# First normalisation in tile groups with an on-chip spread of the condition, and shorter sums of squares at two later norms

## The reference, cut to what matters

```python
mod = silu(c) @ w_ada[l] + b_ada[l]
sh_m, sc_m, gt_m, sh_f, sc_f, gt_f = jnp.split(mod, 6, axis=-1)
h = rms_norm(x, g_mix[l]) * (1.0 + sc_m) + sh_m
proj = jnp.einsum('bsd,de->bse', h, w_in[l])
```

## Time and profile before

| | us |
|---|---|
| median of 3 runs | 795.64 (795.53 to 795.8) |
| the profiled execution, its own time | 795.57 |
| its span | 793.8 |
| PE busy | 751.9 (95%) |
| DVE busy | 649.1 (82%) |
| ACT busy | 387.9 (49%) |
| first matmul of lin 0 starts | 37.61 |

### The profile page before, as it was taken

The page is one execution under the profiler, slowest core; times in us unless marked ns, Lnnn a source line. Parts: engine busy times, 40 slices in busy tenths (PEclk is TensorE's granted clock), DMA queues, the critical chain, the costliest instruction groups (busy, mean ns, idle before and its releaser), DMA issues.

```text
span 793.8 us, 13124 instructions
## 1 busy us (share of the span) xinstructions
PE 751.9 (95%) x5479; PEld 697.9 (88%) x5480; DVE 649.1 (82%) x1001; ACT 387.9 (49%) x521; POOL 46.2 (6%) x31
## 2 busy tenths in 40 slices
PE   0499999999999999999999999999999999999996
PEld 0399999999999999999999998888778899999995
DVE  3988767995897799999898779999989956987752
ACT  2355645557547654544547532322463335365742
POOL 0000000000000422223222000000000000000000
PEclk9799999999999999999999999999999999999998
DMA  9999998765563557766645241313106643563101
GB/s 347 417 352 365 368 348 311 264 223 198 206 240 136 208 212 251 273 246 247 258 175 197 91 176 53 107 55 104 54 0 235 224 148 118 225 231 118 54 1 54
DMA packets 26086, 156.58 MB, mean 197 GB/s; under 512 B 2691, under 2 KB 7084, under 8 KB 7852
## 3 DMA queue, kind: packets, MB, share of 16 engines
q1 hardware_dynamic: 21392, 148.91, 50.5%
q10 hardware_dynamic: 4636, 6.85, 2.6%
HBM read 154.68 MB, written 1.06 MB: 196 GB/s over the span
## 4 chain that ended last, share of the span: by engine, by line
PE 84%; DVE 9%; ACT 3%; issue 1%; ACTq 1%; POOL 1%; DVEq 0%
PE psum L1344 71%; DVE w_lo L832 4%; PE psum L1379 2%; DVE w_lo L865 2%; PE psum L1636 1%; PE psum L1810 1%; PE psum L1786 1%; ACT w_hi L371 1%; PE psum L1798 1%; PE psum L1622 1%; PE psum L1486 1%; DVE arena L1034 1%; DVE arena L1039 0%; PE psum L1601 0%; PE psum L1471 0%
## 5 line engine op out<-in xcount | busy, mean ns | idle before, releaser
L1344 PE MATMUL psum<-h_hi,w_hi 128*128 128x256 f32 (+1 forms) x1312 | 397.2, 303 | 10.2 <-DVE h_lo L905 9.2
L1344 PE MATMUL psum<-h_lo,w_hi 128*128 128x256 f32 (+1 forms) x1312 | 392.1, 299 | 0.0
L1344 PE MATMUL psum<-h_hi,w_lo 128*128 128x256 f32 (+1 forms) x1312 | 392.1, 299 | 0.0
L1344 PEld LDWEIGHTS psum<-h_hi,w_hi 128*128 128x128 f32 x1312 | 251.1, 191 | 21.8 <-issue 11.6
L1344 PEld LDWEIGHTS psum<-h_lo,w_hi 128*128 128x128 f32 x1312 | 251.5, 192 | 7.8 <-issue 0.2
L1344 PEld LDWEIGHTS psum<-h_hi,w_lo 128*128 128x128 f32 x1312 | 251.3, 192 | 7.4
L865 DVE TENSOR_TENSOR w_lo<-raw,w_hi 128x2048 fp32r<-128x2048 f32 x93 | 212.7, 2288 | 50.2 <-ACT w_hi L371 49.4
L371 ACT CAST w_hi<-raw 128x2048 fp32r<-128x2048 f32 x93 | 176.9, 1905 | 20.6 <-DMA raw<-in_w 16.3
L832 DVE SCALAR_TENSOR_TENSOR w_lo<-raw,cond 128x1024 fp32r<-128x1024 f32 x88 | 119.5, 1395 | 8.3 <-PE psum L1344 7.5
L832 DVE SCALAR_TENSOR_TENSOR w_lo<-raw,arena 128x1024 fp32r<-128x1024 f32 x48 | 56.8, 1221 | 0.8
L336 POOL TENSOR_TENSOR arena<-arena 128x512 f32<-128x512 f32 x11 | 26.1, 2370 | 372.9 <-ACT arena L588 372.9
(11 more groups left out here) (214 smaller groups left out, 783.7 us busy)
## 6 DMA issues: line engine op xcount, KB each, us to landing
raw<-in_w SPq DMA_DIRECT2D x141, 1024.0 KB, 4.9
xs<-in_xs ACTq DMA_DIRECT2D x2, 1024.0 KB, 12.0
consts<-diff ACTq DMA_DIRECT2D x8, 128.0 KB, 5.5
cond<-in_cond ACTq DMA_DIRECT2D x1, 1024.0 KB, 6.4
out<-xs SPq DMA_DIRECT2D x4, 256.0 KB, 2.4
arena<-in_cond ACTq DMA_DIRECT2D x1, 512.0 KB, 6.8
consts<-in_c ACTq DMA_DIRECT2D x1, 512.0 KB, 3.4
arena<-in_c ACTq DMA_DIRECT2D x1, 448.0 KB, 3.2
```

The lines of the kernel that those rows point to most:

```text
L1344: last = mm(out, w[a], x[b], start=start and n == 0, stop=stop and n == 2, skip_group_check=skip)
```

## The change

Five things are changed.

1. **Condition.** All three conditions come as one row of 12 KB in one partition. PE spreads them to all partitions by fp32 matmuls with a row of ones (`spread`, 512 columns each). The first two wait for this load and go to banks 0 and 1; ACT applies Silu from there. ACT applies Silu to the other two conditions in the row; four more matmuls spread them later and ACT copies them out. The two broadcast loads (0.5 MB and 1 MB) are gone, and so is a later Silu over 128x2048 with a reload of the function table.
2. **Loads.** ACT's queue issues the condition alone. `xs`, `vec` in two parts, `rel`, `onehot` and `c0` are issued by SP between the chunks; the block of ones is set by POOL. Storing and reloading the position biases moves to after lin 2 and lin 4.
3. **Order.** The mod chunks of scale and shift alternate, one pair for two tiles. `ORDER` begins mod 0 to 3, lin 0, mod 4, mod 5, lin 1, mod 6, mod 7, and goes on as before from lin 2. DVE norms tiles 0 to 3, then 4 and 5, then 6 and 7, and PE takes lin 0 and lin 1 in the pieces tiles 0 to 5 of both, then 6 and 7 of both. 14 bf16 matmuls of zeros (512 columns) stand after the first spread on PE, 14 more before lin 0.
4. **Sums.** For `odd_ctx` DVE adds the squares of tiles 0 to 5 in pairs and PE makes 3 sums in place of 6. For the last norm DVE adds the squares of tiles 0 to 5 into one, and PE makes 3 sums in place of 8, all behind tile 7's matmuls.
5. **Last scaling.** Three multiplies of 3, 3 and 2 tiles in place of eight, and three stores.

```diff
+HEAD = MOD_FIRST + 2
 N_MOD = 48
 LIN_OPEN = 1
-
-ADA_SC_M, ADA_SH_M, ADA_GT_M, ADA_SH_F, ADA_SC_F, ADA_GT_F = 0, 4, 8, 12, 16, 20
+LAST_PARTS = ((0, 3), (3, 6), (6, 8))
+
+ADA_SC_M, ADA_SH_M, ADA_GT_M, ADA_SH_F, ADA_SC_F, ADA_GT_F = 0, 1, 8, 12, 16, 20
...
-    order = [("lin", 0)] + [("mod", m) for m in range(MOD_FIRST)]
+    order = [("mod", m) for m in range(4)] + [("lin", 0), ("mod", 4), ("mod", 5), ("lin", 1), ("mod", 6), ("mod", 7)]
     m = MOD_FIRST
-    for j in range(LIN_BR + 3):
-        order += [("lin", j)] if j else []
+    for j in range(2, LIN_BR + 3):
+        order += [("lin", j)]
...
+        cond_row, ones_row = arena[0:1, 0:3 * D], arena[0:1, 3 * D:3 * D + P]
...
+                if r == 2:
+                    sp.dma_start(xs[:, :, 0:T], xs_d[:, :, 0:T]).then_inc(sem("x_loaded"), 16)
+                elif r == 4:
+                    sp.dma_start(vec[:, 0:VEC["g_ffn"]], vec_d[:, 0:VEC["g_ffn"]]).then_inc(sem("vec_loaded"), 16)
+                elif r == 12:
+                    sp.dma_start(c0[:, 0:P], c0_d).then_inc(sem("c0_loaded"), 16)
+                    sp.dma_start(vec[:, VEC["g_ffn"]:N_VEC], vec_d[:, VEC["g_ffn"]:N_VEC]).then_inc(sem("vec_loaded"), 16)
+                elif r == 6:
+                    sp.dma_start(rel[0:32, :], rel_d).then_inc(sem("rel_loaded"), 16)
+                    sp.dma_start(onehot, c1_d[0:33, 512:896]).then_inc(sem("rel_loaded"), 16)
                 load(r, r % RAW, ORDER[r - RAW] if r >= RAW else None)
 
-            for q in range(4):
-                sp.wait_ge(sem("last_done"), 2 * (q + 1))
-                sp.dma_start(out_d[:, 2 * q:2 * q + 2, :], xs[:, 2 * q:2 * q + 2, 0:T]).then_inc(sem("stored"), 16)
-            sp.wait_ge(sem("stored"), 64)
+            for q, (a, b) in enumerate(LAST_PARTS):
+                sp.wait_ge(sem("last_done"), q + 1)
+                sp.dma_start(out_d[:, a:b, :], xs[:, a:b, 0:T]).then_inc(sem("stored"), 16)
+            sp.wait_ge(sem("stored"), 16 * len(LAST_PARTS))
...
+            pool.memset(c0[:, P:2 * P], 1.0).then_inc(sem("ones_set"), 1)
...
-            act.dma_start(cond_ada, bass.AP(cond_d.tensor, 0, [[0, P], [1, D]])).then_inc(sem("cond_ada_loaded"), 16)
-            act.dma_start(rel[0:32, :], rel_d).then_inc(sem("rel_loaded"), 16)
-            act.dma_start(onehot, c1_d[0:33, 512:896]).then_inc(sem("rel_loaded"), 16)
-            act.dma_start(xs[:, :, 0:T], xs_d[:, :, 0:T]).then_inc(sem("x_loaded"), 16)
-            act.dma_start(c0[:, :], c0_d).then_inc(sem("c0_loaded"), 16)
-            act.dma_start(vec[:, :], vec_d).then_inc(sem("vec_loaded"), 16)
+            act.dma_start(cond_row, bass.AP(cond_d.tensor, 0, [[0, 1], [1, 3 * D]])).then_inc(sem("cond_loaded"), 16)
...
-            act.wait_ge(sem("cond_ada_loaded"), 16)
-            nc.scalar.activation(cond_ada, cond_ada, ACT.Silu).then_inc(sem("cond_ada_ready"), 1)
-            split(0)
-
-            act.wait_ge(sem("bias_row"), 1)
-            nc.scalar.copy(urow, bank[3][0:8, 0:384]).then_inc(sem("bias_row_out"), 1)
-            act.wait_ge(sem("bias_row_out"), 1)
-            act.dma_start(diff_d, urow).then_inc(sem("bias_stored"), 16)
-            act.wait_ge(sem("bias_stored"), 16)
-
+            for n in range(2):
+                act.wait_ge(sem("cond_spread"), n + 1)
+                nc.scalar.activation(cond_ada[:, 512 * n:512 * (n + 1)], bank[n], ACT.Silu).then_inc(sem("cond_ada_ready"), 1)
+            nc.scalar.activation(cond_row[:, D:3 * D], cond_row[:, D:3 * D], ACT.Silu).then_inc(sem("cond_row_ready"), 1)
             def load_trev(h):
 
                 act.dma_start(trev[:, h % TREV, :], bass.AP(diff_d.tensor, 384 * h, [[1, P], [1, T]])
                               ).then_inc(sem(f"trev_loaded{h % TREV}"), 16)
 
-            for h in range(TREV):
-                load_trev(h)
             act.wait_ge(sem("eps_set"), 2)
             load_ln_exp()
             act.wait_ge(sem("x_loaded"), 16)
             for k in range(KT):
                 square("mix", k)
             rstd_of("mix")
-            shift_hi("mix")
+            shift_hi("mix", range(4))
+            split(0)
+            split(1)
+            for v in range(2):
+                act.wait_ge(sem("cond_spread"), 4 + 2 * v)
+                nc.scalar.copy(cond[:, v, :], wide[:, 2 * v:2 * v + 2, :].rearrange("p b n -> p (b n)")
+                               ).then_inc(sem("cond_ready"), 1)
+            shift_hi("mix", (4, 5))
+            split(2)
+            shift_hi("mix", (6, 7))
 
             act.dma_start(consts[:, 0:512], c1_d[:, 0:512]).then_inc(sem("c1_loaded"), 16)
-            split(1)
-
-            act.dma_start(cond.rearrange("p v n -> p (v n)"),
-                          bass.AP(cond_d.tensor, D, [[0, P], [1, 2 * D]])).then_inc(sem("cond_loaded"), 16)
+
             for j in range(LIN_GATE):
-                split(j + 2)
-                if j == 6:
-                    act.wait_ge(sem("cond_loaded"), 16)
-                    nc.scalar.activation(cond[:, :, :], cond[:, :, :], ACT.Silu).then_inc(sem("cond_ready"), 1)
-                    load_ln_exp()
+                if j:
+                    split(j + 2)
...
+                if j == 2:
+                    act.wait_ge(sem("bias_row"), 1)
+                    nc.scalar.copy(urow, bank[3][0:8, 0:384]).then_inc(sem("bias_row_out"), 1)
+                    act.wait_ge(sem("bias_row_out"), 1)
+                    act.dma_start(diff_d, urow).then_inc(sem("bias_stored"), 16)
+                if j == 4:
+                    act.wait_ge(sem("bias_stored"), 16)
+                    for h in range(TREV):
+                        load_trev(h)
...
+            def first_mods(pair):
+
+                for m in range(2 * pair, 2 * pair + 2):
+                    mod(m, RAW_OF_MOD[m] % RAW, 16 * (RAW_OF_MOD[m] // RAW + 1), 2, 2)
+
+            def first_scaled(p0, p1, done, count):
+
+                mod_bias(2 * p0, 2 * p1)
+                n = p1 - p0
+                at = VEC["g_mix"] + 2 * p0
+                scale = modv[:, 8 * p0:8 * p1].rearrange("p (q m t v) -> p q m t v", m=2, t=2, v=2)[:, :, 0, :, 0]
+                out, gain = (z.rearrange("p (q t) -> p q t", t=2) for z in (coef[:, 2 * p0:2 * p1], vec[:, at:at + 2 * n]))
+                nc.vector.scalar_tensor_tensor(out, scale, 1.0, gain, ALU.add, ALU.mult).then_inc(sem(done), 1)
+                dve.wait_ge(sem(done), count)
+                dve.wait_ge(sem("rstd_ready"), 1)
+                for k in range(2 * p0, 2 * p1):
+                    nc.vector.scalar_tensor_tensor(norm_tmp[:, k, :], xs[:, k, 0:T], coef[:, k:k + 1], rstd[:, 0:T],
+                                                   ALU.mult, ALU.mult).then_inc(sem("normed"), 1)
+
+            def first_lo(p0, p1):
+
+                for k in range(2 * p0, 2 * p1):
+                    dve.wait_ge(sem("norm_hi"), k + 1)
+                    nc.vector.scalar_tensor_tensor(h_lo[:, k, 0:T], norm_tmp[:, k, :], shift_col(ADA_SH_M, k),
+                                                   h_hi[:, k, 0:T].bitcast(F32), ALU.add,
+                                                   ALU.subtract).then_inc(sem("norm_lo"), 1)
+
+            dve.wait_ge(sem("cond_ada_ready"), 2)
+            first_mods(0)
+            first_mods(1)
+            dve.wait_ge(sem("vec_loaded"), 16)
+            first_scaled(0, 2, "mix_coef", 1)
+            first_lo(0, 2)
+            mod(4, RAW_OF_MOD[4] % RAW, 16 * (RAW_OF_MOD[4] // RAW + 1), 2, 2)
             split(0)
-            dve.wait_ge(sem("cond_ada_ready"), 1)
-            for m in range(MOD_FIRST):
-                mod(m, RAW_OF_MOD[m] % RAW, 16 * (RAW_OF_MOD[m] // RAW + 1), 1, 1)
-            dve.wait_ge(sem("vec_loaded"), 16)
-            mod_bias(0, 8)
-            coefficients(0, "g_mix", mod_row(ADA_SC_M, 0))
-            norm("mix", 1)
+            mod(5, RAW_OF_MOD[5] % RAW, 16 * (RAW_OF_MOD[5] // RAW + 1), 2, 2)
+            first_scaled(2, 3, "mix_coef", 2)
             split(1)
+            first_lo(2, 3)
+            first_mods(3)
+            first_scaled(3, 4, "coef_ready", 1)
+            first_lo(3, 4)
...
+            for k in (0, 2, 4):
+                dve.wait_ge(sem("sq_odd_ctx"), k + 2)
+                nc.vector.tensor_tensor(gain_sq[:, k, :], gain_sq[:, k, :], gain_sq[:, k + 1, :],
+                                        ALU.add).then_inc(sem("odd_ctx_added"), 1)
...
+            def add_squares(ks):
+
+                for k in ks:
+                    dve.wait_ge(sem("sq_last"), k + 1)
+                    if k > 1:
+                        dve.wait_ge(sem("last_added"), k - 1)
+                    nc.vector.tensor_tensor(norm_tmp[:, 0, :], norm_tmp[:, 0, :], norm_tmp[:, k, :],
+                                            ALU.add).then_inc(sem("last_added"), 1)
...
+                    if k == 3:
+                        add_squares((1,))
+                    if k == 5:
+                        add_squares((2, 3))
+                    if k == 6:
```

(56 more changed lines are left out.)

20 lines of the change are left out of this document (13 added, 7 removed).

## The result

| | before | changed |
|---|---|---|
| median of 4 runs, us | 795.67 (795.53 to 795.8) | 784.45 (784.32 to 785.16) |
| ratio, 95% interval | | 0.9859 [0.9847, 0.9871] |
| the profiled execution / its span, us | 795.57 / 793.8 | 784.45 / 782.6 |
| first mod product of DVE | 15.44 | 8.23 |
| first matmul of lin 0 | 37.61 | 29.32 |

The kernel gained 11.2 us where 11.7 were forecast. What of it each stage gave is read from the chain of waits, at places that both kernels have.

What follows compares the result with a forecast made beforehand. It took the kernel as a head set by DVE's mod products, then 750 us paced by PE. Head 7.8, odd norm 1.3 and end 2.6 sum to 11.7 us off 795.57, giving 783.9 us, range 782.5 to 785.5.

Steps and rivals of the forecast that it cites:

- Head: Start to the end of lin 1: 7.8 us gained, taken between 8.2 by the steps and 6.6 by the other bound.
- odd norm: Context norm's sums on PE: three fewer fp32 sums of 0.43 us each save 1.3 us.
- end: Last norm: six sums between tile 6 and tile 7 leave PE's chain, saving 2.6 us.
- scaling: Last scaling and store: between 0.1 us loss and 0.35 us gain, taken as 0.
- I take 3.3 us: Head: landing of the 12 KB condition row, leading to DVE's first mod product at 7.8 us.
- Mods 0 to 2 take 7.8 to 15.2 us: Head, DVE's order: first three mod products run back to back from 7.8 to 15.2 us.
- [mod 3] lands at 15.5: Head: mod 3, behind 5.25 MB in SP's queue, lands at 15.5 us and is done at 18.0.
- The lower bound's reason: Head: drained ring lands lin 2 at 38.8, its rounding delays tile 6, lin 1 ends at 45.2, gain 6.6 us.
- PE is free at 27.2: Head, before lin 0: PE done with bias matmul and 14 zeros at 27.2 us, 0.8 behind the split, costing nothing.
- the first: Rival, head: the condition lands late, at 7.5 us, and mod 3 ends 3.9 later; 787.8 us, chance 0.08.
- the second: Rival, 60 to 75 us: the weight stream at 365 GB/s is the bound, an earlier PE only waits; 787.4 us, chance 0.08.
- The end pays, the head doesn't: Rival: a later stage where DVE is the pace-maker swallows the head start; 791.7 us, chance 0.05.

Runs made afterwards that it cites:

- the old head: Head of the kernel before (broadcast, order, loads, one group of eight tiles) with points 4 and 5 of the change kept: 792.15 us.
- the edits of the odd norm: Changed kernel with the context norm's sums back to six on PE, without DVE's three additions: 785.84 us.
- the last scaling: Changed kernel with the last scaling back to eight multiplies and four stores: 784.61 us.
- the packed store: Changed kernel with the last scaling written in place to `last_x` and stored from there, in runs of 3 KB, not 1 KB: 784.08 us.
- the one-row matmuls: Changed kernel with the first 14 zeros replaced by three fp32 matmuls of one row: 784.50 us.
- The experiment: Changed kernel with the load of `xs` issued by ACT behind the condition, not by SP between mod 1 and mod 2: 797.03 us.
- both experiments on `xs`: Changed kernel with `xs` issued in ACT's queue, 797.03 us; and with `xs` in SP's queue behind mod 3 in place of mod 1, 789.23 us.

## Why the prediction was right, and which steps were not

**The sum.** Head 7.8 against 7.43 in the chain and 7.5 to 7.7 by the old head; odd norm 1.3 against 1.30 and 1.4; end 2.6 against 2.59 and 2.6; scaling 0 against -0.13, just past the lower bound of -0.1. Each later term was tried alone and held, the head by leaving it out as a whole, and the old head with the new end showed that they add.

**The head by its steps.** The shape was as forecast: DVE bounds it, PE waits at each step between groups, the ring of weights drains when mod 6 waits for the split of lin 0 (157 GB/s from 25 to 30 us). Three sizes were off:

- *"I take 3.3 us"* for the condition: PE began on it at 3.79, and the first product came at 8.23, not 7.8. This had no price, as the next step shows. The estimate of 2.8 us beside the sum was 1.0 short; it came from a fit for loads that POOL issues, and this one is ACT's.
- *"Mods 0 to 2 take 7.8 to 15.2 us", "[mod 3] lands at 15.5"*: mod 2 was waited for (1.16 us) and mod 3 started at 16.78, when it had landed. This is the step that was mis-sized: mod 4, behind the low parts of tiles 0 to 3, began at 22.8, not 21.7. DVE was 0.9 late at the split of lin 0 and 0.7 at mod 6. Then it stood still for 0.53 us before mod 7, though this had landed (34.70), and waited 0.18 for ACT, and tile 6 was there at 41.2 where I had 39.9. These 1.3 us, less what the clock gave back (next point), are the 0.8 by which lin 1 ended after my 43.6. So the steps gave 8.2 where 7.4 were measured, and the 7.8 that I took between the bounds was 0.1 to 0.4 too high. That it was so near is in part luck, since 7.8 is a choice between two bounds. The lower bound's reason (the drained ring brings lin 2 at 38.8) didn't hold: ACT could begin to round lin 2 at 37.21.
- *"PE is free at 27.2"*: it was 29.3. 1.6 us of this is the bias matmul, whose `onehot` was there at 22.6 and not near 21; the rest is the second zeros, of which all but the last two ran at 1.2 GHz. The clock had fallen to 0.50 by 20 us while PE spread the other two conditions. It cost nothing: PE had 24 matmuls to do before a wait, and the pause shrank from my 2.7 us to 1.1. The clock then stayed at full level, so the fall that I had priced didn't come in this execution. That is chance. In three runs with the same head (the edits of the odd norm, of the last scaling and of the packed store) the zeros ran faster, lin 0 began at 27.9 to 28.5, PE paused for 1.85 to 2.31 us, and the clock fell. The Trainium skill, "TensorE: Matmul & The Clock Gate", HAM oscillation, spoke for such a fall. The trace agrees for the longer pauses: it came after 1.75 us without the second zeros (0.52 from 35 to 37.5 us) and after 2.67 us behind the one-row matmuls too, while after pauses of 1.1 to 1.6 us no trace here shows one. In none of the five did it cost more than 0.1 us: without the second zeros and with the one-row matmuls tile 6 was started at 41.32 and 41.27 in place of 41.23, since the wait for it is long enough to hide a burst at the lower level.

Why mod 3 landed at 16.76 and not at 15.5 is open in part. I took the load as landed when 5.25 MB had moved, counted on the rates of the kernel before. The rate isn't at fault. The changed kernel's, in slices of 1.25 us, make 5.08 MB by 15.0 us, where I had 5.04:

```profile
GB/s 0 121 315 406 413 416 351 369 417 419 419 419 411 438 419 426 372 397 419 419 308 7 72 242 439 426 433 419 419 419 413 397 403 423 419 383 392 431 406 400
```

Nor is the time that SP spends on issuing `xs` ahead of mod 2 (1.92 us): with `xs` issued last the same five loads had landed at 16.60. By the rates 5.25 MB had moved near 15.4 us. By the packets the fourth chunk of weights had moved at 15.9, as the sum holds bytes of other loads too. At most the last 0.9 us lie between the last byte and the landing, and no run shows what fills them.

**What I didn't price at all** is where `xs` is issued. I wrote that `xs` "lands near 10.5 us" (11.7 was measured) and took that for granted from its place in SP's queue. The experiment shows that the gain hangs on this place: the condition, the order and the groups without it leave the kernel where it was, with the gains of the later norms used up. It is the exact place that counts, since two chunks further back in the same queue cost 4.8 us. Before the change the same load took 15.8 us and hurt nobody, since its norms began at 35.8; with the norms at 19.7 `rstd` had 2.3 us to spare.

**The rivals.** The condition came at 3.79, not at 7.5: the first falls. The stream carried 387 GB/s with PE busy throughout: the second falls. "The end pays, the head doesn't" falls with the 7.43. The slower rival was wrong about the load, as 12 KB get through, but named a mechanism that the experiment found at work on another: 1 MB in packets of 1 KB in ACT's queue is starved by weights. That its 798.3 is near the 797.03 of the experiment is luck, as it was worked out for another load and another landing.

Open as well are the 0.53 us before mod 7. The profile names no wait for them, and they are the same in both experiments on `xs`, where mod 7 comes 5 and 12 us later.

## What to carry to other kernels

When a stage is pulled forward, list every load that it needs and see which queue each is in: a load with short runs in a queue of its own, beside a stream of long ones, gets its share by packets and not by bytes. Here the queue of one load decided over 12.6 us, more than the head gained. Before warming PE up, look for the engine that is late at that place; 28 dummy matmuls changed the sums from 6.3 to 3.6 us and the kernel not at all. But where the sums are what everybody waits for, the lower clock cost 3 us. Work taken off the path of the bottleneck engine and given to one with slack is safe ground: the sums moved to DVE gave their price to 0.1 us.

## What was not expected of the hardware

- The same load of 1 MB took 22.7 us to landing in a queue of its own beside the weights, and 10.1 us among them.
- Matmuls of one row kept PE busy and didn't raise its clock. After 8.9 us of them the sums took 5.54 us (3.62 after zeros of 128 rows), and in the changed kernel the granted clock fell (0.77, then 0.50) while PE was busy with them for all of 17.5 to 20 us.
- In the first 15 us the granted clock reads 1.00 while matmuls go at the pace of 1.2 GHz (the sums of 6.26 us without zeros). Before the first change of the clock that a trace records, the durations are to be read, not that column.
- A store in runs of 3 KB went at 387 GB/s, in runs of 1 KB at 338 to 345.
- Two multiplies of 128x256 on POOL (1.58 us) stretched the two of DVE's beside them from 0.47 to about 0.95 us each.
